# One stage of a two-block kernel: a bidirectional gated recurrence, by heads instead of by (head, direction) units

## What is computed

```
k, logf = hg_forget(z, lb)        # k = (1-lb) sigmoid(-z), logf = log(lb + (1-lb) sigmoid(z))
b      = cumsum(logf) in a chunk
inter  = (q * exp(b)) @ s                                   # what the state carries in
scores[t, s] = sum_k q[t,k] * exp(b[t,k] - b[s,k]) * k[s,k]   for s <= t
o      = inter + scores @ v
s_new  = exp(b_last) * s + (k * exp(b_last - b))^T @ v
o_total = o_forward + flip(o_backward)                      # the backward pass has its own z, k, b
```

## Time and profile before

| | |
|---|---|
| median of 3 runs | 2602.84 us |
| profiled execution, its own time | 2599.3 us |
| its span | 2597.6 us |
| PE busy | 2484.4 us (96%) |
| DVE busy | 1622.0 us (62%) |
| ACT busy | 886.6 us (34%) |
| POOL busy | 26.8 us (1%) |
| mean granted TensorE clock | 0.992 |

### The profile page before, as it was taken

The page is one execution under the profiler, slowest core; times in us unless marked ns, Lnnn a source line. Parts: engine busy times, 40 slices in busy tenths (PEclk is TensorE's granted clock), DMA queues, the critical chain, the costliest instruction groups (busy, mean ns, idle before and its releaser), DMA issues. The chain is left out here.

```text
span 2597.6 us, 39539 instructions
## 1 busy us (share of the span) xinstructions
PE 2484.4 (96%) x16809; PEld 1336.3 (51%) x16809; DVE 1622.0 (62%) x2112; ACT 886.6 (34%) x1061; POOL 26.8 (1%) x60
## 2 busy tenths in 40 slices
PE   7999889999999999999999999979989999999997
PEld 4457664444444444444767776764434444444443
DVE  6688747544444443645477878786766777774243
ACT  5118316332233232323354544452332222222121
POOL 0010000010000000000000000000000000000000
PEclk9999999999999999999999999999999999999999
DMA  9127563111111124343210000021101211113442
GB/s 328 31 73 235 192 212 131 33 49 49 48 48 48 48 77 111 106 120 130 56 31 18 25 26 25 18 97 50 33 17 52 61 49 48 48 55 106 112 112 87
DMA packets 302918, 207.37 MB, mean 80 GB/s; under 512 B 11296, under 2 KB 298174, under 8 KB 302143
## 3 DMA queue, kind: packets, MB, share of 16 engines
q1 hardware_dynamic: 301910, 205.08, 26.3%
q10 hardware_dynamic: 873, 0.32, 0.1%
HBM read 191.22 MB, written 13.64 MB: 79 GB/s over the span
## 5 line engine op out<-in xcount | busy, mean ns | idle before, releaser
L200 PE MATMUL ps<-hT,arena 128*128 128x512 bf16 (+1 forms) x6240 | 1337.3, 376 | 13.3 <-DVE hT L705 4.9
L200 PEld LDWEIGHTS ps<-hT,arena 128*128 128x128 bf16 x6240 | 609.1, 98 | 739.0 <-issue 17.1
L1917 PE MATMUL ps<-arena 128*128 128x512 bf16 x2112 | 458.7, 379 | 3.0 <-DVE arena L1899 3.0
L1917 PEld LDWEIGHTS ps<-arena 128*128 128x128 bf16 x2112 | 206.3, 98 | 252.2 <-DVE arena L1899 5.3
L2170 DVE SCALAR_TENSOR_TENSOR arena<-ps,vec,arena 128x945 f32<-128x945 f32 (+2 forms) x176 | 215.1, 1222 | 70.1 <-ACT arena L2156 50.7
L2137 DVE SCALAR_TENSOR_TENSOR arena<-ps,vec,arena 128x1023 f32<-128x1023 f32 (+1 forms) x88 | 106.8, 1276 | 177.8 <-ACT arena L2127 177.8
L1899 DVE TENSOR_TENSOR arena<-hT,arena 128x2816 bf16<-128x2816 f32 (+2 forms) x44 | 93.7, 2157 | 164.8 <-ACT arena L1893 164.6
L1893 ACT ACTIVATE arena<-hT 128x2816 bf16<-128x2816 f32 (+2 forms) x44 | 77.8, 1798 | 240.1 <-DMA hT<-w_down_dram 112.6
L2988 PE MATMUL ps<-arena 128*128 128x128 f32 (+1 forms) x896 | 103.2, 272 | 21.6 <-DVE arena L3309 21.6
L2084 DVE TENSOR_TENSOR arena<-hT,arena 128x2048 bf16<-128x2048 f32 x44 | 100.9, 2292 | 28.1 <-ACT arena L2051 27.8
L2988 PEld LDWEIGHTS ps<-arena 128*128 128x128 f32 (+1 forms) x896 | 98.5, 187 | 25.6 <-DVE arena L3309 24.0
(11 more groups left out here) (421 smaller groups left out, 2468.9 us busy)
## 6 DMA issues: line engine op xcount, KB each, us to landing
xT<-ada_w_dram SPq DMA_DIRECT2D x24, 1024.0 KB, 5.9
hT<-w_up_dram SPq DMA_DIRECT2D x44, 512.0 KB, 5.0
hT<-ffn_up_dram SPq DMA_DIRECT2D x44, 512.0 KB, 5.0
hT<-w_down_dram SPq DMA_DIRECT2D x30, 704.0 KB, 7.1
hT<-ffn_down_dram SPq DMA_DIRECT2D x30, 704.0 KB, 6.9
arena<-w_in_dram SPq DMA_DIRECT2D x33, 512.0 KB, 3.9
xT<-w_mod_dram SPq DMA_DIRECT2D x16, 1024.0 KB, 6.1
arena<-w_mod_dram SPq DMA_DIRECT2D x8, 1024.0 KB, 19.2
```

The costliest lines, as they stand in the source:

```text
L200: last = pe.matmul(out, lhs(a, kt), rhs(b, kt, i), start=start and kt == 0 and (a, b) == (0, 0), stop=stop and kt == n_k - 1 and (a, b) == ...
L1917: last = pe.matmul(self.bank(u), self.part(u, a, kt), self.g[:, b, kt, cols], start=kt == 0 and (a, b) == (0, 0), stop=kt == FT - 1 and (a ...
```

## The change

- **Heads instead of units.** PE, ACT and DVE now loop over 4 heads. Both directions of a head are worked on at the same level together: a level has two 1024-column buffers, one for keys (left half forward keys, right half backward keys) and one for queries (left half backward, right half forward). `subtract` writes both (4 operations of 512 elements), ACT takes exp of both (2 of 1024), `weigh` makes two multiplies of 512 and one of 1024, PE makes 8 products per level and head, all of full 128x128 size, and `select` copies all 1024 columns under one mask that holds both directions. The diagonal of both directions is accumulated in PSUM and read once. `att` holds both directions, so the product with the values is made once per head.
- **Order.** For head h, PE runs: turned keys forward, sum of squares of h-1, diagonal, level 0, state products forward, V of h+1, level 1, turned keys backward, carried forward, fill, level 2, state products backward, Z forward of h+1, level 3, carried backward, Z backward of h+1, level 4, QUERY of h+1, level 5, level 6, fill, GATE of h+1, product with the values. Head 0's Z backward and GATE are made ahead of the loop. ACT and DVE have new orders to match (below).
- **Level buffers.** Two instead of three: `subtract(h, l)` waits for the product of level l-2.
- **Weights.** `lo` of tiles 2 to 19 moves from DVE to POOL, which has nothing else to do in this stage. The tile order of heads 1 to 3 is V, Z forward, Z backward, QUERY, GATE.
- **Memory.** Keys and b of even heads move into memory that the late gates used (`scratch_x`); `state0` and `chunk_decay` move into the unused half of `masks`; the late gates' buffers shift.

The core of the diff, per engine (helpers keep their bodies but take `(h, d)` for `n`):

```
-ARENA = 31488
+ARENA = 31744
+    def keys_side(h, l):
+        return x[:, 2 * ((NL * h + l) % 2), :]
+    def queries_side(h, l):
+        return x[:, 2 * ((NL * h + l) % 2) + 1, :]
...
         PE
+            def level(h, l):
+                pe.wait_ge(x_ready, NL * h + l + 1)
+                still, moving = keys_side(h, l), queries_side(h, l)
+                chunk_job((h, "level", l), range(T // P), lambda out, c: pe.matmul(
+                    out, still[:, c * P:(c + 1) * P], moving[:, c * P:(c + 1) * P], start=True, stop=True))
...
+            for piece in (ZF1, V0, V1):
+                front(0, piece)
+            fill(AHEAD)
+            for piece in (ZB0, ZB1, QUERY, GATE):
+                front(0, piece)
+            for h in range(HG_HEADS):
+                turned_keys(h, 0)
+                if h:
+                    sum_of_squares(h - 1)
+                diagonal(h)
+                level(h, 0)
+                state_products(h, 0)
+                front(h + 1, V0)
+                front(h + 1, V1)
+                level(h, 1)
+                turned_keys(h, 1)
+                carried(h, 0)
+                fill(("mid", h))
+                level(h, 2)
+                state_products(h, 1)
+                front(h + 1, ZF0)
+                front(h + 1, ZF1)
+                level(h, 3)
+                carried(h, 1)
+                front(h + 1, ZB0)
+                front(h + 1, ZB1)
+                level(h, 4)
+                front(h + 1, QUERY)
+                level(h, 5)
+                level(h, 6)
+                fill(("end", h))
+                front(h + 1, GATE)
+                pe.wait_ge(selected, h + 1)
...
         ACT
+            for h in range(HG_HEADS):
+                if h:
+                    squares(h - 1)
+                level(h, 0)
+                turned_keys(h, 0)
+                if h:
+                    inverse_root(h - 1)
+                level(h, 1)
+                decays(h, 1)
+                front(h + 1, V0)
+                front(h + 1, V1)
+                weights_hi(h + 1, V1)
+                turned_keys(h, 1)
+                level(h, 2)
+                query_decays(h, 1)
+                level(h, 3)
...
+                front(h + 1, ZF0)
+                front(h + 1, ZF1)
+                softplus_parts(h + 1, 0)
+                weights_hi(h + 1, ZF1)
+                level(h, 4)
+                forget_parts(h + 1, 0)
+                front(h + 1, ZB0)
+                front(h + 1, ZB1)
+                softplus_parts(h + 1, 1)
+                weights_hi(h + 1, ZB1)
+                level(h, 5)
+                front(h + 1, QUERY)
+                weights_hi(h + 1, QUERY)
+                forget_parts(h + 1, 1)
+                level(h, 6)
+                decays(h + 1, 0)
+                query_decays(h + 1, 0)
+                front(h + 1, GATE)
+                weights_hi(h + 1, GATE)
...
+        @block.gpsimd
+        def _(pool):
+            for n in range(2, 5 * HG_HEADS):
+                stream.lo(pool, n)
...
         DVE
+                left, right = halves_of(keys_side(h, l), m)
+                dve.tensor_tensor(left, mid_f, left_f, ALU.subtract)
+                dve.tensor_tensor(right, mid_b, right_b, ALU.subtract).then_inc(sub_done, 1)
+                left, right = halves_of(queries_side(h, l), m)
+                dve.tensor_tensor(left, left_b, mid_b, ALU.subtract)
+                dve.tensor_tensor(right, right_f, mid_f, ALU.subtract).then_inc(sub_done, 1)
...
+                dve.copy_predicated(by_chunk(att), mask, by_chunk(banks(job))).then_inc(read[slot(job)[0]], 1)
...
+            for h in range(HG_HEADS):
+                weigh(h, 0)
+                diagonal(h)
+                select(h, 0)
+                key_distance(h, 1)
+                chain_states(h, 0)
+                weigh(h, 1)
+                decayed_keys(h, 1)
+                decayed_queries(h, 0)
+                subtract(h, 2)
+                if h:
+                    finish(h - 1)
+                select(h, 1)
+                weigh(h, 2)
+                subtract(h, 3)
+                take_fill(("mid", h))
+                select(h, 2)
+                weigh(h, 3)
+                chain_states(h, 1)
+                decayed_queries(h, 1)
+                subtract(h, 4)
+                select(h, 3)
+                softplus(h + 1, 0)
+                weigh(h, 4)
+                subtract(h, 5)
+                forget(h + 1, 0)
+                select(h, 4)
+                weigh(h, 5)
+                subtract(h, 6)
+                softplus(h + 1, 1)
+                select(h, 5)
+                weigh(h, 6)
+                forget(h + 1, 1)
+                key_distance(h + 1, 0)
+                select(h, 6)
+                wait_read(dve, (h, "level", 6))
+                dve.sem_inc(selected, 1)
+                decayed_keys(h + 1, 0)
+                subtract(h + 1, 0)
+                if h < LAST_HEAD:
+                    take_fill(("end", h))
+                scale_q(h + 1)
+                subtract(h + 1, 1)
```

More of the change, by code:

```diff
@@ L2878, in stage_hgrn @@
-    jobs = [(0, "front", piece) for piece in PIECES[0]] + [(-1, "fill", 0)]
-    for n, (h, d) in enumerate(units):
-        def front_of_next(*pieces):
-            return [(n + 1, "front", piece) for piece in pieces if has(n + 1, piece)]
-        jobs += [(n, "kt", 0), (n, "kt", 1), (n, "level", NL), (n, "level", 0), (n, "level", 1)] + \
-                ([(n, "ss", 0)] if d == 0 and h else []) + [(n, "kv", 0), (n, "kv", 1)] + front_of_next(Z0, Z1) + \
-                [(n, "level", 2), (n, "level", 3)] + ([(n, "fill", 0)] if n == last_unit else []) + \
-                front_of_next(V0) + [(n, "level", 4)] + \
-                front_of_next(GATE, V1, QUERY) + [(n, "level", l) for l in range(5, NL)] + \
-                ([(n, "fill", 0)] if n in FILL and n < last_unit else [])
@@ L2888, in stage_hgrn, with keys, b, unit @@
-    jobs.append((last_unit + 1, "ss", 0))
+    LAST_UNIT = 2 * LAST_HEAD + 1
+    def keys(h, d):
+        return odd_keys[:, d, :] if h % 2 else even_keys[d]
+    def b(h, d):
+        return odd_b[:, d, :] if h % 2 else even_b[d]
+    def unit(h, d):
+        return 2 * h + d
+    stream = k.recurrent_weights
+    ZF0, ZF1, ZB0, ZB1, V0, V1, QUERY, GATE = "zf0", "zf1", "zb0", "zb1", "v0", "v1", "q", "g"
+    TILE = {V0: 0, V1: 0, ZF0: 1, ZF1: 1, ZB0: 2, ZB1: 2, QUERY: 3, GATE: 4}
+    def tile_of(h, piece):
+        return 5 * h + (1 - TILE[piece] if h == 0 and TILE[piece] < 2 else TILE[piece])
@@ new lines, in stage_hgrn @@
+    AHEAD = "ahead"
+    FILL = {AHEAD: (0, 0, T), ("mid", 0): (1, 0, 3 * P), ("end", 0): (1, 3 * P, 6 * P), ("mid", 1): (1, 6 * P, T),
+            ("end", 1): (2, 0, 2 * P), ("mid", 2): (2, 2 * P, 4 * P), ("end", 2): (2, 4 * P, 6 * P), ("mid", 3): (2, 6 * P, T)}
+    jobs = [(0, "front", ZF0), (0, "front", ZF1), (0, "front", V0), (0, "front", V1), (AHEAD, "fill"),
+            (0, "front", ZB0), (0, "front", ZB1), (0, "front", QUERY), (0, "front", GATE)]
+    for h in range(HG_HEADS):
+        def front_of_next(*pieces):
+            return [(h + 1, "front", piece) for piece in pieces] if h < LAST_HEAD else []
+        jobs += [(h, "kt", 0, 0), (h, "kt", 0, 1)] + ([(h - 1, "ss")] if h else []) + \
+                [(h, "diagonal"), (h, "level", 0), (h, "kv", 0, 0), (h, "kv", 0, 1)] + front_of_next(V0, V1) + \
+                [(h, "level", 1), (h, "kt", 1, 0), (h, "kt", 1, 1), (("mid", h), "fill"), (h, "level", 2),
+                 (h, "kv", 1, 0), (h, "kv", 1, 1)] + front_of_next(ZF0, ZF1) + [(h, "level", 3)] + \
+                front_of_next(ZB0, ZB1) + [(h, "level", 4)] + front_of_next(QUERY) + [(h, "level", 5), (h, "level", 6)] + \
+                ([(("end", h), "fill")] if h < LAST_HEAD else []) + front_of_next(GATE)
@@ L2890, in slot @@
+    jobs.append((LAST_HEAD, "ss"))
     def slot(job):
@@ L2908, in wait_made, with wait_read @@
         eng.wait_ge(made[s], use + 1)
+    def wait_read(eng, job):
+        s, use = slot(job)
+        eng.wait_ge(read[s], use + 1)
     def x_tokens(t):
@@ L2964, in front @@
                 else:
-                    first, end = {Z0: (0, T), Z1: (T, TT)}.get(piece, (CTX, TT))
+                    first, end = {ZF0: (0, T), ZF1: (T, TT), ZB0: (0, T), ZB1: (T, TT)}.get(piece, (CTX, TT))
                     spans = [(a, min(a + HALF, end)) for a in range(first, end, HALF)]
@@ new lines, in diagonal, with both @@
+            def diagonal(h):
+                pe.wait_ge(k_ready, unit(h, 1) + 1)
+                pe.wait_ge(q_scaled, h + 1)
+                def both(out, c):
+                    for d in range(2):
+                        last = pe.matmul(out, x_tokens(keys(h, d))[:, c * P:(c + 1) * P], q[:, h % 2, c * P:(c + 1) * P],
+                                         start=d == 0, stop=d == 1)
+                    return last
+                chunk_job((h, "diagonal"), range(T // P), both)
```

(2 more changed lines are left out.)

486 lines of the change are left out of this document (183 added, 303 removed).

## The result

The changed kernel takes 2616.97 us (median of 4 runs, 2615.57 to 2617.61), the kernel before 2600.99 (4 runs, 2598.31 to 2603.51). The ratio is 1.0061 with a 95% interval of 1.0043 to 1.0078: slower by 0.6%, 16 us. I had forecast 2602 us, no change, with a range up to 2615. The time lies 2 us above the range.

The account below looks back on a forecast made before the run. TensorE was taken to bound the prologue and heads 0 to 2, not the last unit. -11 + 5.4 + 3.5 + 1.5 = -0.6 us on 2599.3 gave 2598.7, with 3.5 for the median 2602; range 2587 to 2615.

Parts of the forecast that it names:

- TensorE's work: Recurrence: level products halved to some 52 to 58 us, value product made once; 12.8 us less per head, 51 in all.
- Start, +25.6: Prologue: head 0's Z backward and GATE ahead of the loop and forget(0,1) delay the first turned keys to 1349.8, +25.6 us.
- The wait before level 6, 8.9 us: Heads 0 to 2: TensorE waits 8.9 us before level 6 for ScalarE's queued steps and VectorE's wide multiply.
- Heads 0 to 2: Walked length of the heads with a next unit's projections: 107.7 us for head 0, 108.4 each for heads 1 and 2.
- Head 3, 65.5 with 3.5 of clock = 69.0: Last head, a VectorE chain without projections: 65.5 us walked against 88.5 before, plus 3.5 for low clock in its gaps.
- The clock, 1.8 per wait: TensorE's granted clock falls after each 8.9 us wait, costing 1.8 us each, +5.4 for three heads.
- The wide select, 1.2: VectorE's predicated copy of 1024 elements, one for two narrower copies, taken as 1.2 us.
- rival D: VectorE's wide select takes 2.6 us, not 1.2, uncovered in head 3: +10 us, 2612; chance 0.08.
- GpSimd, +1.5: Second parts of weight tiles on GpSimd, 2.6 us each, hold VectorE up by 0 to 1 us per head, 1.5 in all.
- slack of 0.9 us: Time before ScalarE needs sp_ready, taken to absorb part of the GpSimd subtracts' meetings with softplus and weigh 5.
- Sum: Terms -11 + 5.4 + 3.5 + 1.5 = -0.6 us, so 2598.7; the median 3.5 higher, 2602.
- Rival C: GpSimd's second parts hold up VectorE at softplus(h+1, 0) and weigh 5: 4.3 us per head, +9, 2611; chance 0.24.

Follow-up runs that it names:

- e1: Changed kernel with GpSimd's 18 subtracts (second parts of weight tiles 2 to 19) left out, only their signal kept; 2602.5 us, ratio 1.0010 to the kernel before.
- e3: Changed kernel with level 6's work put ahead of the next head's on ScalarE and VectorE, second parts still on GpSimd; 2585.2 us, ratio 0.9945 to the kernel before.
- e9: Changed kernel with only ScalarE's level 6 exponentials moved right behind level 5's, VectorE's order kept; 2606.0 us, ratio 1.0017 to the kernel before.
- e6: Changed kernel with 44 extra products of constants on TensorE ahead of level 6 in heads 0 to 2; 2611.9 us, ratio 1.0036 to the kernel before.
- e7: e4 with the first fill moved behind the backward gate's fronts and ScalarE's turned keys ahead of the squares; 2590.8 us, ratio 0.9956 to the kernel before.
- e4: Changed kernel with e3's order and the second parts of the weights back on VectorE; 2583.6 us, ratio 0.9941 to the kernel before.

## Why the prediction was wrong, point by point

- **TensorE's work: right.** The level products, forecast at 52 to 58 us, took 68.8, but eight of their 28 groups ran at a low clock and took 3.32 to 3.79 us for 2.05, 12.9 us more in all. At full clock that is 56.
- **Start, +25.6, first keys at 1349.8: right but for GpSimd.** e1 1350.8, changed kernel 1353.3. These executions enter the stage up to 1.1 us apart, so the distance from the first product of V of head 0 tells more: 34.1 before, forecast 59.7, 59.9 in e1 and 63.6 in the changed kernel.
- **The wait before level 6, 8.9 us: confirmed.** 8.82, 8.82 and 8.15 us in e1. Its cause, ScalarE's and VectorE's queue, is shown by e3 and e9.
- **Heads 0 to 2: right but for GpSimd.** 107.7, 108.4 and 108.4 with 1.8 of clock each are 329.9 us; e1 has 109.9 + 111.1 + 109.8 = 330.8, the changed kernel 340.9.
- **Head 3, 65.5 with 3.5 of clock = 69.0:** 71.0 in the changed kernel and 71.2 in e1. Here two terms were mis-sized against each other. Level 1, levels 3 to 6 and the value product took 3.3 to 3.8 us each instead of 2.05, 9.5 us in all rather than 3.5; if all of it lies on the chain, the walk was some 4 us too long without it. That the two errors nearly cancel is luck. No run keeps the clock up in head 3, but e9, whose code for head 3 is the same, points that way: there the six rows lose 7.0 us instead of 9.5, and the head takes 68.9 instead of 71.0. The last such row, 3.79 for the 2.05 of the earlier trace rows:

```profile
1761.45 3.79 PE L3084 MATMUL ps<-arena 128*128 128x128 f32 x16 [1.44 <-DVEq L3472]
```

- **The clock, 1.8 per wait: a little small.** The mechanism of the earlier trace rows held after all three waits (granted clock 0.50 in level 6 each time); the low level reached into the fill (4.43 for 4.06), and e6 measured 2.0 to 2.5 per head.
- **The wide select, 1.2: 1.31 measured,** so rival D (2.6) is excluded.
- **GpSimd, +1.5: the step that failed.** It costs 14.5 us (e1). The length of a subtract was bounded well (2.6 taken, 2.31 on average, 2.13 alone). What was wrong is the claim that "VectorE is waiting for ScalarE anyway while three of the five lo's of a head run", and the slack of 0.9 us set against the other two. Against e1, the wait before level 6 grows by 3.6 in heads 0 and 1 (12.4 for 8.8): weigh 5 is longer by 1.1 and the last operation of softplus by 1.9, on a meeting that the walk had not put there at all, that of QUERY's second part with softplus(h+1, 1). VectorE also comes 1.3 later against ScalarE: from the start of weigh 5 to the end of the weight copy are 8.05 us instead of 9.32, which fits the earlier meeting with softplus(h+1, 0). Some 0.8 is slack: 1.1 + 1.9 + 1.3 - 0.8 = 3.5, the idle time that ScalarE's row shows. Head 2 bears this out: it has no QUERY subtract (the last of the 18 starts at 1657.3), its softplus keeps 0.82 us, and its wait grows by 2.4 only (10.52 for 8.15), the 1.1 and the 1.3. The start, for which the forecast had no term, loses 3.7 more: 1.8 in softplus(0, 1) and 1.9 in the scans of forget(0, 1).
- **Sum.** Without GpSimd the forecast would have been 2600.5, and e1 took 2602.5. The sum also added 3.5 us for the distance of the median from the profiled execution; with the 2601.0 of this result that is 1.7. Rival C had the cause and its two places in the heads right, but not QUERY's and not the start. Its own price, 4.3 per head, is 12.9 for three heads, near the 14.5 measured, but it went into its forecast as 9 above the 1.5 already taken, 10.5 in all; it had a chance of 0.24. The rule of the Trainium skill that I had set against the change (SBUF — State Buffer, "SBUF: two separate sides": VectorE and GpSimd hold a shared port pair exclusively, the loser blocks for the whole instruction, and VectorE's operations in its two-port mode are held as those with two SBUF inputs are) agrees with these rows. By it each of the 18 subtracts may cost VectorE up to its whole 2.13 us, an estimated 38 us in the stage; and by its GPSIMD Engine Reference, section 3.1, a subtract takes an estimated 2.2 us, which the row of 2.13 bears out. I let a walk with slacks below 1 us overrule it.

Open: what e7's two moves cost apart; how much of head 3's low clock lies on the chain; and a version with second parts on GpSimd only in VectorE's idle stretches wasn't tried. The fastest kernel with the whole computation is e4, 2583.6 us, 0.6% under the kernel before; e3, which differs from the change only in the order of level 6, is as good.

## What to carry to other kernels

Work given to GpSimd is no relief for VectorE if it is made of SBUF operations that run beside VectorE's: price each at up to its whole length on VectorE's chain (here 2.1 us), and look for the row that it will meet, not for VectorE's idle share. When two products are merged into one, look at what the hand-written order puts between the last of them and its inputs: here the next head's QUERY copy, weight copy and forget exponentials on ScalarE, and its softplus on VectorE, stood ahead of level 6, and moving level 6's work in front of them was worth 32 us. A long wait of TensorE cost its length and then 2.0 to 2.5 us more for the low clock behind it.

## What the runs showed of the hardware

- A GpSimd subtract of 128x1024, f32 to bf16, takes 2.13 to 2.15 us where VectorE is idle as it starts, against 1.22 us on VectorE; 2.31 on average in the changed kernel, since it is held off where VectorE's operation was first (2.71 for the one that started 0.7 us before the end of L3287).
- VectorE's operation that meets it is held off nearly until it ends: by 1.8 us with 1.95 of the subtract left (3.30 for 1.49), by 1.1 with 1.2 left (2.38 for 1.29), and with one tensor input from SBUF as well, by 1.9 with 2.1 left (2.74 for 0.82). A predicated copy from PSUM was not: those that started 0.2 us after a subtract took 1.33 and 1.34 us.
- After 7 to 15 us without a product the next group of eight took 3.5 to 3.8 us for 2.05, and the fill behind it was in part longer; in the changed kernel the granted clock of these groups was 0.50 in heads 0 to 2. With products of constants in the wait it stood at 1.00. A short wait can go either way: in e3 1.95 us of it were followed by 3.24 us for level 6 in head 0 and by 2.05 in heads 1 and 2.
- A predicated copy of 128x1024 from PSUM takes 1.29 to 1.34 us, at every level; those of 512 took up to 1.32 each.
